# Expert weights of gate and up in strips of 1024 columns over two PSUM banks each

## What is computed

```python
def swiglu(x, w_gate, w_up, w_down):
    return (jax.nn.silu(x @ w_gate) * (x @ w_up)) @ w_down

def moe_swiglu(xn, w_router, we_gate, we_up, we_down):
    logits = (xn @ w_router).astype(jnp.float32)
    top_v, top_i = lax.top_k(logits, TOP_K)
    ...
    y = jnp.zeros_like(xn)
    for e in range(N_EXPERTS):
        y = y + gates[..., e:e + 1].astype(xn.dtype) * swiglu(xn, we_gate[e], we_up[e], we_down[e])
```

## Time and profile before

| | us |
|---|---|
| median of 3 runs (1438.14 to 1439.49) | 1439.26 |
| the profiled execution, its own time | 1435.77 |
| its span, first to last instruction | 1434.0 |
| TensorE matmuls busy in it | 1407.8 (98%) |
| VectorE busy | 1193.1 (83%) |
| ScalarE busy | 1036.8 (72%) |
| mean granted TensorE clock | 0.996 of full |

### The profile page before, as it was taken

The page is one execution under the profiler, slowest core; times in us unless marked ns, Lnnn a source line. Parts: engine busy times, 40 slices in busy tenths (PEclk is TensorE's granted clock), DMA queues, the critical chain, the costliest instruction groups (busy, mean ns, idle before and its releaser), DMA issues.

```text
span 1434.0 us, 21439 instructions
## 1 busy us (share of the span) xinstructions
PE 1407.8 (98%) x6803; PEld 1174.7 (82%) x6803; DVE 1193.1 (83%) x1545; ACT 1036.8 (72%) x1367; POOL 54.4 (4%) x107
## 2 busy tenths in 40 slices
PE   9999999999999999999999999999999999999998
PEld 8998888888888788888888878888878888887786
DVE  6968645544588799999989989989999998998896
ACT  6766544444487677888888888878888878888784
POOL 1000000000010100000000010000001000001000
PEclk9999999999999999999999999999999999999999
DMA  8554555555153599999999999999999999999994
GB/s 301 165 195 160 186 189 193 178 196 172 57 209 121 211 376 382 377 358 391 379 349 395 396 383 394 393 382 382 395 394 384 393 397 368 396 396 383 394 393 165
DMA packets 192175, 442.07 MB, mean 308 GB/s; under 512 B 8862, under 2 KB 20476, under 8 KB 192124
## 3 DMA queue, kind: packets, MB, share of 16 engines
q1 hardware_dynamic: 188924, 429.89, 81.4%
q0 software_dynamic: 3168, 11.54, 2.8%
q10 hardware_dynamic: 32, 0.01, 0.0%
HBM read 433.54 MB, written 7.86 MB: 308 GB/s over the span
## 4 chain that ended last, share of the span: by engine, by line
PE 73%; DVE 10%; DMA 8%; issue 5%; ACT 3%; DVEq 0%; SPq 0%; ACTq 0%
PE bank L556 70%; DVE w_lo L1885 7%; DMA raw<-in_we_down_dram 5%; ACT w_hi L1338 1%; DMA raw<-in_we_gate_dram 1%; PE bank L1185 1%; DMA raw<-in_we_up_dram 1%; DMA raw<-in_w_mem_kv_dram 1%; DVE qkT L2008 1%; PE bank L901 0%; PE bank L568 0%; DVE aT_hi L2616 0%; DVE act_f L2607 0%; PE bank L1164 0%; DVE xT_lo L1929 0%
## 5 line engine op out<-in xcount | busy, mean ns | idle before, releaser
L1885 DVE TENSOR_TENSOR w_lo<-raw,w_hi 128x1024 fp32r<-128x1024 f32 (+2 forms) x832 | 955.0, 1195 | 140.5 <-ACT w_hi L1338 133.1
L1338 ACT ACTIVATE w_hi<-raw 128x1024 fp32r<-128x1024 f32 (+2 forms) x832 | 832.1, 1041 | 227.8 <-PE bank L556 176.0
L556 PE MATMUL bank<-w_hi,xT_hi 128*128 128x512 f32 (+3 forms) x1358 | 527.9, 389 | 6.1 <-DVE w_lo L1885 4.2
L556 PE MATMUL bank<-w_hi,xT_lo 128*128 128x512 f32 (+3 forms) x1358 | 521.2, 384 | 0.0
L556 PE MATMUL bank<-w_lo,xT_hi 128*128 128x512 f32 (+3 forms) x1358 | 520.0, 383 | 0.0
L556 PEld LDWEIGHTS bank<-w_hi,xT_hi 128*128 128x128 f32 x1358 | 255.1, 188 | 56.1 <-DVE w_lo L1885 4.7
L556 PEld LDWEIGHTS bank<-w_hi,xT_lo 128*128 128x128 f32 x1358 | 254.9, 188 | 49.1
L556 PEld LDWEIGHTS bank<-w_lo,xT_hi 128*128 128x128 f32 x1358 | 255.3, 188 | 46.2
L556 PE MATMUL bank<-w_hi,aT_hi 128*128 128x512 f32 x544 | 218.7, 402 | 8.8 <-DVE aT_hi L2616 8.1
L556 PE MATMUL bank<-w_lo,aT_hi 128*128 128x512 f32 x544 | 217.7, 400 | 0.0
L556 PE MATMUL bank<-w_hi,aT_lo 128*128 128x512 f32 x376 | 148.7, 396 | 0.0
(11 more groups left out here) (392 smaller groups left out, 740.3 us busy)
## 6 DMA issues: line engine op xcount, KB each, us to landing
raw<-in_we_gate_dram SPq DMA_DIRECT2D x112, 1024.0 KB, 9.1
raw<-in_we_up_dram SPq DMA_DIRECT2D x112, 1024.0 KB, 8.7
raw<-in_we_down_dram SPq DMA_DIRECT2D x112, 1024.0 KB, 9.5
raw<-in_w_gate_dram SPq DMA_DIRECT2D x14, 1024.0 KB, 5.1
raw<-in_w_up_dram SPq DMA_DIRECT2D x14, 1024.0 KB, 5.0
raw<-in_w_down_dram SPq DMA_DIRECT2D x14, 1024.0 KB, 4.7
raw<-in_w_in_dram SPq DMA_DIRECT2D x16, 768.0 KB, 5.4
raw<-in_w_out_dram SPq DMA_DIRECT2D x8, 1024.0 KB, 6.2
```

Source lines behind the costliest of these rows:

```text
L556: return pe.matmul(o, a, b, start=start, stop=stop, skip_group_check=True, **kw)
L1338: act.activation(split_piece(w_hi, c, shape, half), raw_piece(c, shape, half), ACT.Copy).then_inc(hi_ready, 1)
L1885: dve.tensor_tensor(split_piece(w_lo, c, shape, half), raw_piece(c, shape, half), F(split_piece(w_hi, c, shape, half)), ALU.subtract).then ...
```

## The change

gate and up are fetched and multiplied in strips of 1024 columns (WC) where there were two of 512. A chunk is then two blocks of 128 rows by 1024 columns (shape WROW, rows of 4 KB, 14 KB apart), a piece one block by 1024 columns, and e_in_wide gives its first 512 columns to one bank and the others to a second: gate to banks 0 and 6, up to 1 and 7. There are three wide strips (WIDE) and the seventh small one of 512 columns, as before. The two parts of a wide strip are turned one after the other through bank 2, the second behind half of the next up, once e_low has emptied the bank; aT_hi and aT_lo are seen as eight blocks (eT), and e_down takes eight blocks. In pieces: gate and up of the first wide strip 0 to 15, two steps of 24 (8 gate, 8 up, 8 down), the small strip's gate and up 64 to 71, down of the last wide strip 72 to 79, the last down 80 to 83. Bytes, matmuls, transposes, splits, silu and products are as many as before.

```diff
...
+    WIDE = (NF - 1) // 2
+    WC = 2 * FC
...
+        WROW = (2, WC)
...
+        blocks = lambda t: t[:, :, :].rearrange("p q (r s) -> p (q r) s", r=2)
+        eT = (blocks(aT_hi), blocks(aT_lo))
+        GATE_BANKS, UP_BANKS = (0, 6), (1, 7)
+        WIDE_STEP = 3 * WC // FC * 2
+        SMALL = 8 + WIDE_STEP * (WIDE - 1)
...
             def expert(e, more, c0=C_MOE):
...
+                gate, up = (w.rearrange("e (j k p) n -> j e p k n", j=4, p=P) for w in (we_gate1, we_up1))
+                small = [w.rearrange("e (j k p) n -> j e p k n", j=2, p=P) for w in (we_gate1, we_up1)]
+                down = we_down1.rearrange("e (f j k p) n -> j e f p k n", j=2, k=2, p=P)
+                here = bass.ds(e, 1)
+                def wide(c, n, more):
+                    for w in (gate, up):
+                        for j in range(4):
+                            src = w[j, here, :, :, bass.ds(n * WC, WC)].rearrange("a p k n -> (a p) k n")
+                            fetch(c, WROW, src, more)
+                            c += 1
+                def down_rows(c, f, more):
+                    for j in range(2):
+                        fetch(c + j, DOWN, down[j, here, bass.ds(f, 1)].rearrange("a b p k n -> (a b p) k n"), more)
+                wide(c0, 0, more)
+                with sp.Fori(0, WIDE - 1) as i:
+                    m = more + WIDE_STEP * i
+                    wide(c0 + 8, i + 1, m)
+                    down_rows(c0 + 16, 2 * i, m)
+                    down_rows(c0 + 18, 2 * i + 1, m)
+                c = c0 + SMALL
+                for w in small:
+                    for j in range(2):
+                        src = w[j, here, :, :, (NF - 1) * FC:NF * FC].rearrange("a p k n -> (a p) k n")
+                        fetch(c, UP, src, more)
+                        c += 1
+                for n, f in enumerate((NF - 3, NF - 2, NF - 1)):
+                    down_rows(c + 2 * n, f, more)
...
+            def e_in_wide(c, banks, more, gathered=None, inside=None):
+                for k in range(KD):
+                    if gathered is not None and k % 4 == 0:
+                        pe.wait_ge(sem("gather_ready"), gathered + k // 4 + 1)
+                    pe.wait_ge(lo_ready, 2 * c + k + 1 + 2 * more)
+                    w = [split_piece(x, c + k // 2, WROW, k % 2) for x in wS]
+                    for half in range(2):
+                        for a, b in TERMS:
+                            last = mm(B[banks[half]][:, :], xT[a][:, k, 0:P], w[b][:, 0, half * FC:(half + 1) * FC],
+                                      start=(k == 0 and (a, b) == (0, 0)), stop=(k == KD - 1 and (a, b) == TERMS[-1]))
+                    last.then_inc(piece_used, 1)
+                    if inside and k == KD // 2 - 1:
+                        inside()
+            def e_turn(n, t, half):
                 pe.wait_ge(sem("eact_done"), n + 1)
+                if half == 1:
+                    pe.wait_ge(sem("eaT_ready"), t)
                 for q in range(FB):
-                    last = pe.transpose(B[2][:, q * P:(q + 1) * P], act_f[:, q * P:(q + 1) * P], ident[:, :])
+                    b = half * FB + q
+                    last = pe.transpose(B[2][:, q * P:(q + 1) * P], act_f[:, b * P:(b + 1) * P], ident[:, :])
                 last.then_inc(sem("eaT_psum"), 1)
...
-            def e_down(c, more, n, start, stop, narrow):
+            def e_down(c, more, t, start, narrow):
                 terms = down_terms(narrow)
-                pe.wait_ge(sem("eaT_ready"), n + 1)
-                for j in range(4):
+                for j in range(2 * FB):
+                    if j % FB == 0:
+                        pe.wait_ge(sem("eaT_ready"), t + j // FB + 1)
                     pe.wait_ge(lo_ready, 2 * c + j + 1 + 2 * more)
                     w = [split_piece(x, c + j // 2, DOWN, j % 2) for x in wS]
                     for half in range(2):
                         for a, b in terms:
-                            last = mm(B[4 + half][:, :], aT[a][:, j, 0:P], w[b][:, 0, half * 512:(half + 1) * 512],
-                                      start=(start and j == 0 and (a, b) == (0, 0)),
-                                      stop=(stop and j == 3 and (a, b) == terms[-1]))
+                            last = mm(B[4 + half][:, :], eT[a][:, j, :], w[b][:, 0, half * 512:(half + 1) * 512],
+                                      start=(start and j == 0 and (a, b) == (0, 0)), stop=False)
                     last.then_inc(piece_used, 1)
...
             def unit(u, narrow=False, last=False):
-                more, n0 = FFN_CHUNKS * u, NF * u
-                e_in(C_MOE + 2, 1, more)
+                more, n0, t0 = FFN_CHUNKS * u, NF * u, (NF - 1) * u
+                e_in_wide(C_MOE + 4, UP_BANKS, more)
                 def e_step(i, start):
...
+                    m = more + WIDE_STEP * i
+                    n, t = n0 + 2 * i, t0 + 2 * i
+                    pe.wait_ge(sem("esilu_done"), n + 2)
+                    e_in_wide(C_MOE + 8, GATE_BANKS, m)
+                    e_turn(n, t, 0)
+                    e_in_wide(C_MOE + 12, UP_BANKS, m, inside=lambda: e_turn(n + 1, t + 1, 1))
+                    e_down(C_MOE + 16, m, t, start, narrow)
                 e_step(0, True)
                 if last:
                     turn_rows()
                 else:
                     turn_next(u)
-                with pe.Fori(1, NF - 1) as i:
+                with pe.Fori(1, WIDE - 1) as i:
                     e_step(i, False)
+                n, t, c = n0 + NF - 3, t0 + NF - 3, C_MOE + SMALL
+                pe.wait_ge(sem("esilu_done"), n + 2)
+                e_in(c, 0, more, None)
+                e_turn(n, t, 0)
+                e_in(c + 2, 1, more, lambda: e_turn(n + 1, t + 1, 1))
+                e_down(c + 4, more, t, False, narrow)
                 e_turn_halves(n0 + NF - 1)
                 if not last:
                     gathered_turned(u + 1)
-                e_down_end(C_MOE + 40, more, u, last, narrow)
+                e_down_end(c + 8, more, u, last, narrow)
                 if last:
                     back(u - (NE - 1))
                     return
-                e_in(C_MOE + FFN_CHUNKS, 0, more, gathered=2 * u + 2)
+                e_in_wide(C_MOE + FFN_CHUNKS, GATE_BANKS, more, gathered=2 * u + 2)
                 pe.wait_ge(sem("y_scaled"), 2 * u + 2)
             keep_busy(6, 6)
...
+                def pieces(a, b, m=more, lp=lap):
+                    for j in range(a, b):
+                        split_high(p0 + j, WROW, m, lp)
+                pieces(4, 13)
                 keep_gate(u)
                 act.wait_ge(sem("turned"), u + 1)
...
+                e_silu(C_MOE + 4, more, None, 2)
+                pieces(13, 24)
+                with act.Fori(0, WIDE - 1) as i:
+                    m, lp = more + WIDE_STEP * i, lap + 2 * i
+                    pieces(24, 29, m, lp)
+                    e_high(t0 + 2 * i, 0, narrow)
+                    e_silu(C_MOE + 12, m, n0 + 2 * i + 2, 2)
+                    pieces(29, 33, m, lp)
+                    e_high(t0 + 2 * i + 1, 1, narrow)
+                    pieces(33, 48, m, lp)
+                p, n, t = 2 * SMALL, n0 + NF - 3, t0 + NF - 3
+                pieces(p + 8, p + 9)
+                e_high(t, 0, narrow)
+                e_silu(C_MOE + SMALL + 2, more, n + 2, 1)
+                pieces(p + 9, p + 11)
+                e_high(t + 1, 1, narrow)
+                pieces(p + 11, p + 20)
                 for b in range(2):
                     act.wait_ge(sem("eaT_half_psum"), 2 * u + b + 1)
-                    cols = slice(0, HALF_SLOTS if narrow else P)
-                    act.activation(aT_hi[:, 2 * b:2 * b + 2, cols],
-                                   B[(2, 6)[b]][:, 0:2 * P].rearrange("p (q s) -> p q s", q=2)[:, :, cols], ACT.Copy).then_inc(sem("eaT_half_hi"), 1)
+                    high_part(2 * b, 2, B[(2, 6)[b]], narrow).then_inc(sem("eaT_half_hi"), 1)
                 if not last:
                     for j in (0, 1):
...
                 next_narrow = not narrow and not first
+                def pieces(a, b, m=more):
+                    for j in range(a, b):
+                        split_low(p0 + j, WROW, m)
+                pieces(6, 8)
                 if first:
-                    split_low(p0 + 6, UP, more)
                     rank_experts()
-                    split_low(p0 + 7, UP, more)
+                pieces(8, 10)
+                if first:
                     order_units()
-                    split_low(p0 + 8, UP, more)
+                pieces(10, 12)
+                if first:
                     unit_products()
-                    split_low(p0 + 9, UP, more)
+                pieces(12, 14)
+                if first:
                     unit_tables()
...
+                pieces(14, 21)
+                e_product(C_MOE + 8, more, n0, 2)
+                pieces(21, 24)
                 if not last:
```

(21 more changed lines are left out.)

106 lines of the change are left out of this document (32 added, 74 removed).

## The result

The changed kernel takes 1447.66 us (median of 4 runs, 1446.29 to 1449.62), the kernel before on the same chip 1438.78 us (4 runs, 1438.14 to 1439.49): a ratio of 1.0063, with a 95% interval of 1.0045 to 1.0080. It is 8.9 us slower, where 7 us faster was forecast. The profiled execution is that of 1446.29 us.

A forecast was written before the change was run, and what follows sets the result against it. TensorE plus its few stalls was taken to bound the expert stage, with VectorE and DMA also full. Gains of 4.2 (narrow ends), 2.0 (unit 7) and 1.0 (first unit) took 1439.3 to 1432.1 us, range 1426.5 to 1442.

The forecast's parts named there:

- Part 1: Expert weight fetches: 4 KB rows raise gate and up from 387 to 402 GB/s; ScalarE's DMA waits nearly vanish.
- rival (c): Expert fetches: rate follows contiguity of down's block, not row length, and stays at 387 GB/s; 1442.7 us, slower; chance 0.13.
- Part 2: Gate and up matmuls switching PSUM bank every three: cost taken as 0, bounds 0 and +14 us.
- Part 3: Down eight pieces at a time: narrow ends stall 2.9 us plus 0.2 restarts each, 9.3 against 13.5; 4.2 us gained.
- Part 4: Work moved: unit 7's waits go, 2.0 us gained; first unit's waits fall from 2.1 to 1.05 us, 1.0 gained.
- The sum, 7.2 us,: Whole kernel: 4.2 at narrow ends, 2.0 in unit 7 and 1.0 in the first unit, giving 1432.1 us.
- The change keeps all of it, so only stalls can move: Expert stage: TensorE's matmuls and transposes stay, 16.94 us a wide strip and 15.07 narrow; only its stalls can change.
- (d): Narrow steps: the 0.4 us margin at piece 40 is missing; stalls in each, or full 14 us; 1440 to 1453; chance 0.11.
- what was taken from the earlier trace: Narrow ends: TensorE's clock survives 1.40 us of idleness, falls after 2.27 to 3.13; at 1.65 no lowered clock taken.

The follow-up runs named there:

- the two fetches by halves: Changed kernel, outer loops written out, each expert chunk fetched by two DMAs: wide gate/up chunks with 2 KB rows 1449.90 us, with 4 KB rows 1427.93 us.
- the control: The kernel before with the outer loop over units 1 to 6 written out on ScalarE, VectorE and TensorE: 1437.76 us, ratio 0.9998.
- the last experiment: Changed kernel, outer loops written out, one activation low part moved ahead of the low part of weight piece 72: 1432.88 us, ratio 0.9968.

## Why the prediction was wrong

Step by step, by the order of the prediction:

- **Part 1, right in kind and larger.** 410 GB/s among gate and up where 402 was taken; the bound was 420. ScalarE's waits for DMA fell as said. What it is worth was mis-sized: rival (c) put a rate of 387 at 1442.7, 10.6 us above the forecast and 3.4 above before, and the two fetches by halves show 22.0 us and 12.1 above the control. (c) priced only the narrow ends; at 387 the DMA engines are full from there to the end (share 1.05), and TensorE also stands in the wide units behind them, 0.8 us before 870.54 and 0.9 us before 1106.97.
- **Part 2, right.** xT matmuls stay 0.227 us apart (838.82 to 841.53, twelve of them), and down's 0.233.
- **Part 3, right.** 1.1 + 1.8 us with 0.2 for restarts were forecast for each narrow end, 0.93 + 1.71 came in after and 0.99 + 1.59 without the loops, and the clock stayed at full. So 13.5 became 7.8, not 9.3: 1.5 us more gain.
- **Part 4, right.** Unit 7's waits are gone; the first unit keeps 0.35 us of its 2.1, where 1.05 was forecast.
- **The sum, 7.2 us,** against 8.8 us of the change without its jumps: near, with the sign right. That it is so near is in part luck: the rate came out above what was taken, and the sum has no term for what the new order loses or gains by the rate.

**The step that failed** stands at the head of the working: "The change keeps all of it, so only stalls can move", with a sum that has a term for each wait in the strips and none for the program's own length. The diff writes a strip out in two parts, with small strips and half turns of their own, and the body of the outer loop carries that twice, once for each of its two units. The bodies grow from 228 to 338 instructions (ScalarE) and from 555 to 1243 (TensorE), and at these lengths the jumps back, which cost nothing before, stop both engines. By whole times, each taken against before on its own chip, that cost 17.5 us (8.9 slower in place of 8.6 faster); by S it is 19.2 us. No rival had this mechanism: (d) was the nearest in time, 1440 to 1453, and it was not what happened. The trace of before could not show the price, as its pause there is none; but it held the place (a jump twice in the stage, at which all three engines depend on each other within two pieces), and the diff held the growth.

As to the clock, what was taken from the earlier trace rows held: 1.41 to 1.58 us of idleness before the last down left it at full (1.00) at all 33 narrow ends of the eleven kernels with the changed order and 4 KB rows that have such an end. Behind the pauses at the jumps (2.4 to 4.0 us) it fell at some (0.50 in 850 to 854 us of the run with TensorE's loop kept) and not at others (1.00 in 1086 to 1090 of the same run), and behind the 2.24 us of the last experiment at one end of three. The other half of that step, that it falls after 2.27 us and more, did not hold as a rule: behind 2.78 us of idleness at the control's third narrow end (before 1301.76) the clock stayed at 1.00, and with 2 KB rows it fell behind 1.90 us (before 1057.65), to 0.57 in 1058 to 1062 us:

```profile
1302.00:1306.00 4.00, 4.00 (x18) 3.24 (x18) 4.00 (x10) 4.00 (x11) 0.00 (x0) 1.00 1.05 388
```

```profile
1058.00:1062.00 4.00, 4.00 (x13) 3.21 (x12) 3.42 (x4) 2.70 (x4) 0.05 (x1) 0.57 1.05 388
```

## What to carry to other kernels

When a change writes loop steps out, or unrolls, count each engine's instructions in every loop that encloses it, and look in the profile at the branch itself and at the engines' first work behind each jump back: a branch of microseconds, or a gap labelled "issue" there, with more instruction packets, is a price that no sum over the work contains. It may go away by writing the outer loop out, by a shorter body, or by moving the loop some tens of instructions, which for ScalarE here was worth 12 us. And compare a change with its control in the same form: the same change was +8.9 us with loops and -8.8 us without. Here the changed kernel without TensorE's and ScalarE's outer loops (1427.9 to 1429.9 us) is faster than both.

## What was not expected of the hardware

- A long jump back stops ScalarE for 5.2 to 5.7 us, or not at all, by length and place. TensorE's branch takes 6.1 to 6.4 us (0.21 with the short body), of which the matmuls already issued hide all but 1.4 to 3.0. VectorE with 333 instructions never stood at its jump, in any run.
- The wait is not always named: TensorE's pause at its own jump is labelled with VectorE's low part in three runs and with "issue" in one. What gave it away was that VectorE and ScalarE had nothing to do meanwhile, and that it stayed when their loops were gone.
- Rows of 4 KB in place of 2 KB raise one core's rate from 387 to 410 GB/s, with the same number of DMAs and bytes; doubling the number of DMAs changes neither rate (410 and 409 in 1040 to 1050 us) nor time (1427.93 and 1428.93 us).
- What stays open: how many blocks TensorE and VectorE can jump back over, whether TensorE's and VectorE's jumps depend on the place as ScalarE's do (no run moved theirs), and why data come late in unit 7 of the run with ScalarE's loop kept.
